# A hybrid encoder step on one core: the modulation products of layer 0 with their operands swapped

## The reference, cut to what matters

```python
mod = silu(c) @ w_mod[l] + b_mod[l]            # c: (1, 1024), one for the prompt, one for the sample
sh1, sc1, g1, sh2, sc2, g2 = jnp.split(mod[:, None, :], 6, axis=-1)
hn = _rms_norm(x, P['norm_mix_g'][l]) * (1.0 + sc1) + sh1
...
x = x + g1 * y
hn = _rms_norm(x, P['norm_ffn_g'][l]) * (1.0 + sc2) + sh2
x = x + g2 * _swiglu(hn, P['w_ffn_in'][l], P['w_ffn_out'][l])
```

## Time and profile before

| | us |
|---|---|
| median of 3 runs | 1761.63 |
| the runs | 1761.23 to 1773.27 |
| span of the profiled execution | 1768.1 |
| TensorE busy in it (share) | 1591.9 (90%) |
| VectorE busy | 917.1 (52%) |
| ScalarE busy | 518.3 (29%) |

### The profile page before, as it was taken

The page is one execution under the profiler, slowest core; times in us unless marked ns, Lnnn a source line. Parts: engine busy times, 40 slices in busy tenths (PEclk is TensorE's granted clock), DMA queues, the critical chain, the costliest instruction groups (busy, mean ns, idle before and its releaser), DMA issues.

```text
span 1768.1 us, 30493 instructions
## 1 busy us (share of the span) xinstructions
PE 1591.9 (90%) x11260; PEld 1516.8 (86%) x11260; DVE 917.1 (52%) x1652; ACT 518.3 (29%) x780; POOL 128.7 (7%) x148
## 2 busy tenths in 40 slices
PE   6899998998998999999967898888897999999997
PEld 5898898898998899999957787666696999999997
DVE  3835446354786568648775444443456333333344
ACT  2223424332321112222243333322324222222233
POOL 0000000000121012102100000000000100100000
PEclk9988898888999999999988897886898999999999
DMA  8223233334353345435312111111022232232222
GB/s 267 81 82 115 66 106 89 98 95 131 107 155 123 113 133 154 143 95 153 100 35 62 40 48 33 33 33 33 16 72 60 83 95 83 84 95 83 84 80 78
DMA packets 228556, 160.69 MB, mean 91 GB/s; under 512 B 9802, under 2 KB 216348, under 8 KB 228380
## 3 DMA queue, kind: packets, MB, share of 16 engines
q1 hardware_dynamic: 215916, 115.11, 22.7%
q0 software_dynamic: 12288, 44.85, 7.9%
q10 hardware_dynamic: 304, 0.10, 0.0%
HBM read 156.46 MB, written 3.57 MB: 91 GB/s over the span
## 4 chain that ended last, share of the span: by engine, by line
PE 73%; DVE 13%; issue 6%; ACT 5%; DMA 1%; DVEq 1%; SPq 0%; ACTq 0%
PE ring L544 56%; PE core_j L431 5%; DVE param_rows L464 3%; PE core_j L488 2%; DVE weight_low L408 1%; ACT weight_high L403 1%; PE core_j L743 1%; PE core_k L748 1%; PE core_k L1189 1%; DVE normed_low L636 1%; PE core_k L1106 1%; DMA mixer_area<-in_x_sample 1%; PE ring L1166 1%; PE core_k L1109 1%; PE ring L1799 0%
## 5 line engine op out<-in xcount | busy, mean ns | idle before, releaser
L544 PE MATMUL ring<-normed_high,weight_high 128*128 128x272 f32 x2128 | 468.5, 303 | 53.7 <-DVE normed_low L636 30.1
L544 PE MATMUL ring<-normed_high,weight_low 128*128 128x272 f32 x2128 | 456.4, 297 | 0.0
L544 PE MATMUL ring<-normed_low,weight_high 128*128 128x272 f32 x2128 | 456.4, 297 | 0.0
L544 PEld LDWEIGHTS ring<-normed_high,weight_high 128*128 128x128 f32 x2128 | 352.9, 199 | 62.6 <-issue 45.4
L544 PEld LDWEIGHTS ring<-normed_low,weight_high 128*128 128x128 f32 x2128 | 352.5, 198 | 0.0
L544 PEld LDWEIGHTS ring<-normed_high,weight_low 128*128 128x128 f32 x2128 | 349.6, 198 | 0.0
L408 DVE TENSOR_TENSOR weight_low<-weight_raw,weight_high 128x1024 fp32r<-128x1024 f32 x197 | 256.9, 1306 | 72.5 <-ACT weight_high L403 68.4
L403 ACT ACTIVATE weight_high<-weight_raw 128x1024 fp32r<-128x1024 f32 x197 | 206.2, 1050 | 182.9 <-PE ring L544 166.3
L544 PE MATMUL ring<-mixed_high,weight_high 128*128 128x272 f32 x960 | 206.6, 297 | 11.9 <-DVE weight_low L408 8.0
L544 PE MATMUL ring<-mixed_low,weight_high 128*128 128x272 f32 x960 | 202.8, 293 | 0.0
L544 PE MATMUL ring<-mixed_high,weight_low 128*128 128x272 f32 x960 | 202.6, 293 | 0.0
(11 more groups left out here) (373 smaller groups left out, 1358.8 us busy)
## 6 DMA issues: line engine op xcount, KB each, us to landing
weight_raw<-in_w_ffn_in SPq DMA_DIRECT2D x88, 512.0 KB, 3.9
mod_weight<-in_w_mod POOLq DMA_DIRECT2D x48, 512.0 KB, 4.2
mod_weight<-in_w_mod POOLq DMA_DIRECT2D x18, 1024.0 KB, 5.8
weight_raw<-in_w_ffn_out SPq DMA_DIRECT2D x32, 512.0 KB, 3.6
weight_raw<-in_a_w_in SPq DMA_DIRECT2D x24, 512.0 KB, 3.9
weight_raw<-in_c_w_in SPq DMA_DIRECT2D x20, 512.0 KB, 3.9
mixer_area<-in_w_mod SPq DMA_DIRECT2D x6, 1024.0 KB, 12.4
weight_raw<-in_w_ffn_out SPq DMA_DIRECT2D x16, 384.0 KB, 3.1
```

Source lines behind the costliest of these rows:

```text
L544: last = pe.matmul(PS[p.slot][:, half, 0:HALF], w[n.slot][:, k, :], x[:, k, half * HALF:(half + 1) * HALF], start=(k == 0 and w is WH and ...
```

## The change

For groups 8 to 23 of layer 0 the operands change places. `CSW` is silu(c) widened to 32 columns per tile, two of them filled and 30 zero. It is stationary, in a strip of 32 columns of the array, and the modulation weights stream, 256 columns a matmul: 8 matmuls in place of 16. The result is two rows of 256 features, in 32 partitions of `MRPS`, PSUM columns 256 to 511 of the same bank. VectorE copies them to `MROW` in SBUF, and two small matmuls with a selector (`FOLD`: a 1 at row 0 of the first column, at row 1 of the second) turn them into the four columns of `MODPS` as before.

The product of group g + 1 is made where the columns of group g are made, so the product is one group ahead. The first, group 8, is issued in front of the head loop, and its copy stands in VectorE's queue in front of the first norm. The scores and the key-value products wait for the copy. The output product gets loops of its own (`out0_pe`, `out0_dve`) with the last step outside, which has no further product. GpSimd asks for group g when the rows' product of g - 1 is done.

```diff
+        CSW = sb("silu_c_wide", [P, KD, 32])
+        MROW = ROWS[:, 0:2, :].rearrange("p m n -> p (m n)")
...
-        MODPS = J[:, 1, 256:260]
+        MODPS = J[:, 1, 192:196]
+        MRPS = J[:, 1, 256:512]
...
+        def mod_rows(pe, g):
+
+            pe.wait_ge(s_mw, g * 16 + 16 * (1 - MG_DIRECT))
+            for k in range(KD):
+                mm = pe.matmul(MRPS[0:32], CSW[:, k, :], MW[:, k, :], start=(k == 0), stop=(k == KD - 1))
+            mm.then_inc(s_mrows, 1)
+
+        def mod_fold(pe, g):
+
+            for s in range(2):
+                mm = pe.matmul(MODPS[:, 2 * s:2 * s + 2], MROW[0:32, s * P:(s + 1) * P], FOLD[0:32], start=True, stop=True)
+            mm.then_inc(s_modu, 1)
+
+        def mod_next(pe, g, more=True):
+
+            pe.wait_ge(s_mrc, g - MG_NORM + 1)
+            if more:
+                mod_rows(pe, g + 1)
+            mod_fold(pe, g)
+
+        def mod_copy(dve, g):
+
+            dve.wait_ge(s_mrows, g - MG_NORM + 1)
+            dve.tensor_copy(MROW[0:32, :], MRPS[0:32]).then_inc(s_mrc, 1)
...
+        def out0_pe(pe):
...
+            def step(i, end=False):
+                for j in range(2):
+                    project(pe, Turn(W_OUT0, j, 2, i), Turn(R_OUT0, j, 2, i), KD, (GH, GL), mixed=(s_glo, KD))
+                mod_next(pe, i + 20, not end)
...
@@ gpsimd
-            with pool.Fori(MG_NORM, MOD_TILES // 2) as g:
-                pool.wait_ge(s_modu, g - MG_DIRECT)
-                pool.sem_inc(s_half, 1)
+            pool.wait_ge(s_modu, MG_NORM - MG_DIRECT)
+            load_mod(pool, 0, lambda: MG_NORM)
+            with pool.Fori(MG_NORM + 1, MOD_TILES // 2) as g:
+                pool.wait_ge(s_mrows, g - MG_NORM)
+                pool.sem_inc(s_note, 1)
                 load_mod(pool, 0, lambda: g)
@@ tensor
+            pe.wait_ge(s_cs, 2)
+            pe.wait_ge(s_mod, MG_NORM)
+            mod_rows(pe, MG_NORM)
+            pe.wait_ge(s_cst, 16)
             with pe.Fori(0, HEADS) as h:
...
-                mod_group(pe, 3 * h + MG_NORM)
+                mod_next(pe, 3 * h + MG_NORM)
                 item(2, 2)
                 pe.wait_ge(s_qt, h + 1)
-                pe.wait_ge(s_mod, 3 * h + MG_NORM + 1)
+                pe.wait_ge(s_mrc, 3 * h + 2)
...
@@ vector
             dve.tensor_scalar(CS[:, :, :], CS[:, :, :], 0.5, None, ALU.mult).then_inc(s_cs, 1)
+            st.done(dve.memset(CSW[:, :, :], 0.0))
+            dve.wait_ge(s_cs, 1)
+            dve.tensor_copy(CSW[:, :, 0:2], CS[:, :, :].rearrange("p c k -> p k c")).then_inc(s_cs, 1)
             clear_sum(dve)
...
             mod_add(dve, J[:, 1, 0:4 * MG_NORM], 0, MG_NORM).then_inc(s_mod, MG_NORM)
+            mod_copy(dve, MG_NORM)
             dve.wait_ge(s_mod, MG_NORM)
             norm_dve(dve, 0, Turn(R_N0), 0, KD, cols1("norm_mix_g", KD), rstd=False)
...
                 mod_read(dve, 3 * h + MG_NORM)
+                mod_copy(dve, 3 * h + MG_NORM + 1)
                 lo_of(dve, w(3))
```

More of the change, by code:

```diff
@@ L59 @@
 C_MASK = C_NEG + P
-C_ALL = C_MASK + P
+C_SEL = C_MASK + P
+C_ALL = C_SEL + 2
 EARLY_BUFS = 5
@@ L108, in constants @@
     c[:, C_MASK:C_MASK + P] = (l >= s) & (l // 64 == s // 64)
+    for j in range(4):
+        c[32 * j, C_SEL] = c[32 * j + 1, C_SEL + 1] = 1.0
     return c
@@ L174, in encoder @@
         CHUNK_MASK = CST[:, C_MASK:C_MASK + P].bitcast(U32)
+        FOLD = CST[:, C_SEL:C_SEL + 2]
         ONES = sb("ones", [P, P])
@@ L718, in out_pe @@
                 if group is not None:
-                    mod_group(pe, group + i, step == 4)
+                    mod_group(pe, group + i)
+        def out0_pe(pe):
+            pe.wait_ge(s_glo, KD - 1)
+            def step(i, end=False):
+                for j in range(2):
+                    project(pe, Turn(W_OUT0, j, 2, i), Turn(R_OUT0, j, 2, i), KD, (GH, GL), mixed=(s_glo, KD))
+                mod_next(pe, i + 20, not end)
+            with pe.Fori(0, KD // 2 - 1) as i:
+                step(i)
+            step(KD // 2 - 1, True)
         def ffn_pe(pe, w0, p0, glo, group, q):
@@ L917, in out_dve, with out0_dve, step @@
                 step(n, True)
+        def out0_dve(dve):
+            clear_sum(dve)
+            def step(i, end=False):
+                for j in range(2):
+                    lo_of(dve, Turn(W_OUT0, j + 1, 2, i))
+                    residual_dve(dve, Turn(W_OUT0, j, 2, i), Turn(R_OUT0, j, 2, i), 2 * KD, i * 2 + j)
+                    add_square(dve, 1, i * 2 + j, j)
+                mod_read(dve, i + 20)
+                if not end:
+                    mod_copy(dve, i + 21)
+            with dve.Fori(0, KD // 2 - 1) as i:
+                step(i)
+            step(KD // 2 - 1, True)
         def ffn_dve(dve, w0, p0, done, gate, q, group, last=False):
@@ L1867, in _ @@
                 head_var(pe, OSQ, s_osq, h)
-                mod_group(pe, 3 * h + MG_NORM + 2)
-            out_pe(pe, W_OUT0, R_OUT0, KD, s_glo, KD, 20)
+                mod_next(pe, 3 * h + MG_NORM + 2)
+            out0_pe(pe)
             norm_pe(pe, 1, Turn(R_N1))
@@ L2058, in _ @@
                 mod_read(dve, 3 * h + MG_NORM + 1)
+                mod_copy(dve, 3 * h + MG_NORM + 2)
                 lo_of(dve, w(5))
@@ L2107, in _ @@
             st.end(HEADS)
[L2108 removed]
+            out0_dve(dve)
             lo_of(dve, Turn(W_FFN0 + 1))
```

38 lines of the change are left out of this document (18 added, 20 removed).

## The result

The changed kernel is slower: 1779.38 us, median of 8 runs (1774.21 to 1794.65), beside 1765.8 us of the kernel before in 8 runs. The ratio is 1.0078, with a 95% interval from 1.0041 to 1.0115. The forecast was 1761 us and "the same"; the time lies inside the range given, in its upper third, and 18 us above the forecast. The change is small, 0.8%, but the interval sets it apart from no change.

What follows compares the result with a forecast made beforehand. TensorE was taken to bound the kernel, its clock falling behind the groups. The loop's 14.7 us won and the prologue's 13.9 lost made -0.8, from 1761.6 to about 1761 us, "same"; range 1749 to 1774, widened to 1790.

Steps and rivals of the forecast that it cites:

- The prologue: Before the head loop: first norm waits for group 8's copy, product and weights, starting 13.9 us later (bounds 11.3 to 14.8).
- The price of a group: Each modulation group after the change: strip product, selector product and shape changes take 4.3 us, against 3.47 before.
- I take it that the clock holds: At the groups: 256-column streams leave TensorE only some 0.7 us of short work, so the clock does not fall.
- The rest of a head hangs on VectorE and ScalarE and holds the third group off the chain.: In each head, only two groups count on the chain; four heads go from 159.30 to 147.3 us, 12.0 won.
- the sum: Whole kernel: loop 14.7 us won, prologue 13.9 lost, together -0.8 us.
- the clock that the groups lose: Before the change, half-clock time cost 18.7 us in the four heads and 4.6 in the output product.
- the issue gap: Skill's rule for the eight strip matmuls: 1.75 us; the prediction kept the measured row's 3.44 instead.
- The forecast's own range: The main forecast's time range, 1749 to 1774 us, given a chance of 0.68.
- a strip that loses the clock between the projections: Rival: strip products do not hold the clock in heads, output product and prologue; +25, 1787 us; chance 0.22.
- The signs that the prediction named for being right: Head stretches' clock near 1.00, projections 6.1 us behind groups, matmuls about 0.43, groups 4.3, first norm near 83.
- R: Time of one group's strip and selector products with shape changes: 4.3 us, bounds 3.9 to 4.8.
- the loop: Four heads and output product: 12.0 plus 2.7, 14.7 us won; bounds 19 and 5.

Runs made afterwards that it cites:

- rows_in_loop: Changed kernel with each head's first strip product issued behind that head's first projection, nothing of group 8 before the first norm: 1767.66 us, ratio 0.9989.
- early_load: Changed kernel with GpSimd asking for group 8's weights in front of its memsets: 1773.96 us, ratio 1.0022 to the kernel before.
- fill_idle: Changed kernel plus four unread 512-column fp32 streams on TensorE behind each head's third group: 1767.64 us, ratio 1.0010 to the kernel before.
- two_ahead: Changed kernel with second group's strip product at the head boundary, group 8's copy behind the first norm, gate matmuls repeated behind key-value products: 1745.21 us, ratio 0.9867.
- before_short_third: Kernel before the change with each head's third modulation group cut from 32 matmuls to 4 (values wrong, timing only): 1776.04 us, ratio 1.0027.
- best: two_ahead plus early_load's edit plus two unread streams before the output product's wait for the last mixed tile: 1741.83 us, ratio 0.9826 to the kernel before.
- fill_tail: Changed kernel with each head's first gate matmuls repeated, unread, in the idle time behind the key-value products: 1769.92 us, ratio 1.0007.

## Why the prediction was wrong

**The prologue** was right in mechanism and nearly in size: 12.1 us for 13.9. The weights came 1.1 us earlier than forecast, the product took 5.58 instead of 6.0. rows_in_loop and early_load show that it is the copy in VectorE's queue, and the load behind the memsets at the head of that chain.

**The price of a group** was right: 4.10 us for 4.3. **"I take it that the clock holds"** was right for the groups, where the prediction asked it: 6.2 us behind every one.

**The step that failed is "The rest of a head hangs on VectorE and ScalarE and holds the third group off the chain."** It is true of the kernel before. What failed is what the sum made of it: it put the stretches between the heads at nothing and left each head's second projection at its full-clock length, as if the change could not reach either. But the sum had counted the clock that the groups lose, and the third group loses clock as well. Before the change it did so off the path: half of the first projection of the next head ran at half clock (8.9 us in all), took up TensorE's spare time, and the clock was back when the second projection began. The change gave that projection its clock back, and the idle behind it grew by 2.4 us (4.06 less 1.62); the engine then stood still where it had been slow, and the fall moved onto the path. That took 8.1 us back (26.97 us for three second projections instead of 18.85), which is why heads 1 to 3 together won nothing, 117.92 for 117.93 us, while head 0, which has no boundary in front, won what was forecast. fill_idle, two_ahead and before_short_third show this from three sides. The output product's second projection lost 1.5 us in the same way (7.74 for 6.29): its first projection has its clock back too, and TensorE's wait for the last mixed tile grew from 0.28 us to 2.40. The two streams in best, in that wait, brought it back.

The second part of the miss is the stretch behind the key-value products, where nothing was forecast: +6.3 us in the four. The clock falls in or just behind a wait of 1.87 us that was as long before. fill_tail shows that a stream in that wait prevents it. Why the wait did not cost the clock in heads 0, 1 and 3 before, and did in head 2, is not settled, so here the cause stays open: in fill_idle the same wait with the same work around it cost it in head 0 throughout, in heads 1 and 2 for a part, and in head 3 not at all, so there the moment does have a part.

The two misses are 8.1 + 6.3 = 14.4 us; without them the changed code would have won 3.8 us instead of losing 10.6, on the forecast's side of zero and 3 us from its -0.8. The profile of before had the evidence: a projection of 8.9 us off the path behind the third group, with only 1.62 us of idle time behind it. The Trainium skill's "TensorE: Matmul & The Clock Gate", section HAM oscillation — how this bites in real kernels, describes a loop whose every step begins at the lower clock because TensorE waits in front of it; the trace agrees (8.92 us behind 4.06 us of idle time, and in fill_idle 6.28 behind 0.63). The prediction should have weighed that page where it weighed the issue gap.

That 1779 us lies inside the stated range is luck. The forecast's own range ended at 1774; it was drawn out to 1790 for a strip that loses the clock between the projections, and it does not. The signs that the prediction named for being right looked mainly at the projections behind the groups, and those came; only the granted clock of heads 1 to 3, 0.92 instead of near 1.00, pointed at the miss. One bound was added up wrongly, without effect on the forecast: with R = 4.8 and 6 us of falls left the loop wins 14.7 - 11 x 0.5 - 6, about 3 us and not 5.

## What to carry to other kernels

When work in front of a wait gets shorter, because there is less of it or because it has its clock back, ask what TensorE does in the time that is left: idle time there can have a price, paid in clock by the next work behind the wait, and the wait's own end does not show it. Look for real work that may be moved into such a wait (here the next group's product, 3.57 us a head and the clock besides) before filling it with work that nothing reads. And a copy that is made ahead of time for a pipeline must not stand in an in-order queue in front of work that is urgent; issue the first step of the pipeline inside the loop, or behind that work.

## What the runs showed of the hardware that was not expected

A stream through 32 columns of the array took as long per column as one through 128: 0.223 us for an instruction of 256 fp32 columns beside 0.43 for one of 512. Between two projections it held the clock: the projection behind took 6.20 to 6.23 us in every head. At the head boundary it did not always (5.26 us for a product in best).

The clock was kept over 0.48, 0.63 and 1.62 us of idle time in front of a head's second projection; over 4.06 and 7.85 us it was lost, by the end of the wait or about a microsecond later. At 1.87 us, with short products behind it, both were seen. The length of one wait alone does not settle it: 1.73 us in front of the output product's second projection came with 6.29 us in best and with 8.58 in two_ahead, where TensorE had stood another 2.41 us shortly before.

Less work made a kernel slower (before_short_third, 1.0027), and more work made one faster (fill_idle, 1.0010 where the changed kernel has 1.0078).

Code that no edit touched took from 1306.1 to 1325.9 us in single executions. For a change in the first quarter of this kernel the beginning of the next untouched stage is the finer measure: two profiles of the unedited changed kernel agree there within 0.3 us, although the places of their slow clock differ a little.
